# Gated delta layer, back stage: order of the gate weight loads on SyncE and of the state update on VectorE

## What is computed

```python
def step(s, xs):
    q_c, k_c, u_c, w_c, qk_c, sd_c = xs
    v_new = u_c - jnp.einsum('bhck,bhkv->bhcv', w_c, s)
    o_c = jnp.einsum('bhck,bhkv->bhcv', q_c, s) + jnp.einsum('bhij,bhjv->bhiv', qk_c, v_new)
    s = s * sd_c[..., None, None] + jnp.einsum('bhck,bhcv->bhkv', k_c, v_new)
    return s, o_c
...
gate = jax.nn.silu(z.reshape(bsz, t, GDN_V_HEADS, GDN_HEAD_V).astype(jnp.float32))
o = rms_norm(o, norm_w) * gate
```

## Time and profile before

| | us |
|---|---|
| median of 3 runs (lowest, highest) | 3392.73 (3389.57, 3393.57) |
| profiled execution, whole | 3392.64 |
| its span, first to last instruction | 3390.8 |

### The profile page before, as it was taken

The page is one execution under the profiler, slowest core; times in us unless marked ns, Lnnn a source line. Parts: engine busy times, 40 slices in busy tenths (PEclk is TensorE's granted clock), DMA queues, the critical chain, the costliest instruction groups (busy, mean ns, idle before and its releaser), DMA issues. The chain is left out here.

```text
span 3390.8 us, 41168 instructions
## 1 busy us (share of the span) xinstructions
PE 2907.4 (86%) x15594; PEld 2543.9 (75%) x15594; DVE 1855.7 (55%) x3342; ACT 1207.2 (36%) x2080; POOL 642.0 (19%) x386
## 2 busy tenths in 40 slices
PE   5787659969999999899999997998566768699987
PEld 4787438868898989898888886877455558588877
DVE  4324443327997988577788785449223333444433
ACT  3323442223225776333333333663133331222221
POOL 0002110002332333364233230430111110000000
PEclk8898789989999999999999998999778879899999
DMA  2102012133435888899999995572533322222222
GB/s 106 61 15 77 2 50 87 62 127 132 143 112 195 296 311 292 315 397 364 355 362 359 355 360 183 175 224 95 156 89 94 96 72 94 100 99 99 98 89 81
DMA packets 248691, 574.56 MB, mean 169 GB/s; under 512 B 43776, under 2 KB 152192, under 8 KB 217312
## 3 DMA queue, kind: packets, MB, share of 16 engines
q1 hardware_dynamic: 209808, 430.24, 37.8%
q0 software_dynamic: 36864, 134.23, 10.2%
q10 hardware_dynamic: 1872, 8.13, 0.7%
HBM read 486.39 MB, written 86.11 MB: 169 GB/s over the span
## 5 line engine op out<-in xcount | busy, mean ns | idle before, releaser
L40 PE MATMUL pe_ps<-hh,pe_uh 128*128 128x384 f32 x1024 | 352.5, 344 | 21.7 <-issue 17.7
L41 PE MATMUL pe_ps<-hl,pe_uh 128*128 128x384 f32 x1024 | 346.6, 338 | 0.0
L42 PE MATMUL pe_ps<-hh,pe_ul 128*128 128x384 f32 x1024 | 346.3, 338 | 0.0
L40 PE MATMUL pe_ps<-pe_vh,pe_whi 128*128 128x512 f32 x768 | 299.5, 390 | 3.0 <-DVE pe_vl L1498 3.0
L41 PE MATMUL pe_ps<-pe_vl,pe_whi 128*128 128x512 f32 x768 | 299.3, 390 | 0.0
L42 PE MATMUL pe_ps<-pe_vh,pe_wlo 128*128 128x512 f32 x768 | 299.3, 390 | 0.0
L1325 POOL DMA_INDIRECT pe_gu<-in_u_rows,pe_urow x128 | 198.2, 1548 | 316.4 <-DVE pe_gu L1459 289.8
L1333 POOL DMA_INDIRECT pe_gv<-in_v_w,pe_vrow x128 | 155.6, 1216 | 333.3 <-DVE pe_acc L1468 318.8
L40 PEld LDWEIGHTS pe_ps<-hh,pe_uh 128*128 128x128 f32 x1024 | 196.1, 191 | 24.0 <-issue 23.7
L40 PE MATMUL sc_ps<-hh,sc_wh 128*128 128x512 f32 x512 | 200.5, 392 | 13.0 <-DVE sc_wl L2695 13.0
L1459 DVE SCALAR_TENSOR_TENSOR pe_gu<-pe_gu,pe_xs 128x1024 f32<-128x1024 f32 x128 | 155.2, 1219 | 91.6 <-DMA pe_gu<-in_u_rows,pe_urow 91.2
(11 more groups left out here) (479 smaller groups left out, 7197.2 us busy)
## 6 DMA issues: line engine op xcount, KB each, us to landing
xu<-in_u_w SPq DMA_DIRECT2D x64, 1024.0 KB, 6.6
pe_v_raw<-in_v_w SPq DMA_DIRECT2D x64, 1024.0 KB, 8.4
sc_raw<-in_sc_w SPq DMA_DIRECT2D x32, 1024.0 KB, 4.9
hidden_scratch<-pe_hs SPq DMA_DIRECT2D x64, 384.0 KB, 8.9
gate_scratch<-pe_stage SPq DMA_DIRECT2D x24, 1024.0 KB, 11.1
pe_hw<-hidden_scratch SPq DMA_DIRECT2D x64, 384.0 KB, 4.7
pe_gate<-gate_scratch SPq DMA_DIRECT2D x64, 384.0 KB, 5.3
mrg_raw<-in_mrg_w SPq DMA_DIRECT2D x16, 1024.0 KB, 4.8
```

The lines of the kernel that those rows point to most:

```text
L40: pe.matmul(out, lh, rh, start=start, stop=False)
L41: pe.matmul(out, lh, rl, start=False, stop=False)
L42: return pe.matmul(out, ll, rh, start=False, stop=stop)
```

## The change

On SyncE, the load of gate weight tile 2 is issued at the end of the prologue, and the later ones two chunks sooner than before, at the head of an odd chunk's work in front of its two chunk loads. On VectorE, `state(1, g-1)` is issued in front of `merge`.

```diff
@@ gdn_back, block.sync
                     load_u(l, B)
                     load_rc(2 + l)
                     load_at(l, B)
+                load_z(2)
                 for g in range(LAST):
                     c, i = g // NCH, g % NCH
+                    if i % 2 and g // 2 + 3 < 2 * KH:
+                        load_z(g // 2 + 3)
                     if g + 3 < LAST:
                         load(0, g + 3)
                         load(1, g + 3)
-                    if i % 2 and g // 2 + 2 < 2 * KH:
-                        load_z(g // 2 + 2)
                     if g % B == 1 and 2 * B <= g + 7 < LAST:
@@ gdn_back, block.vector
                     rest(0, g)
+                    if g:
+                        state(1, g - 1)
                     if due(c, i) is not None:
                         merge(due(c, i))
-                    if g:
-                        state(1, g - 1)
                     rest(1, g)
```

## The result

The changed kernel takes 3277.0 us (median of 4 runs, 3273.09 to 3281.2) against 3391.43 us of the kernel before beside it (4 runs, 3389.57 to 3393.57). The ratio is 0.9663, 95% interval 0.9646 to 0.9679: 3.4% less, 114 us. The profiled execution has a span of 3273.0 us against 3390.8.

The account below looks back on a forecast made before the run. Late gate weights stalling ScalarE, and so TensorE, were taken as the bound: 3392.7 us less 109.6 (114.1 from idle time and lower clock, less 4.5 for a new `ub` wait) gave 3283 us, range 3273 to 3306.

Parts of the forecast that it names:

- The bound: ScalarE waits 89.1 us in 14 pieces at `high` for gate weights asked for too late, idling TensorE 70.9 us.
- The clock's part: In the back stage's loop, matmuls at the lower clock level after gaps cost 30 us, which would go.
- The rival by which the clock stays low: Only idle time in the loop goes, the 30 us of slower matmuls stay: 3313 us, chance 0.05.
- The loop without stalls: From `solve` of chunk 0 to that of chunk 31, 215.1 us instead of 329.2, summed from undisturbed stretches.
- two bare chunks: Two chunks without corner and merge took 11.10 us, so each chunk's base was put at 5.55 us.
- ScalarE's longest chain: After `gate`: `high`, table load, root, corner and hand-over take 3.2 us, ending 0.3 us before TensorE is ready for `merge`.
- rival (a): Other ScalarE and VectorE queue work replaces the stalls, 14 to 28 us back: 3297 to 3311 us, chance 0.20.
- The wait that appears: In chunk 2 of a head, merge waits for late `ub` loads: 1.3 to 3.1 us three times, 4.5 taken.
- Slower: Weights in front delay the chunk loads, TensorE waits at `carry` for `pk_in`: 3479 us for 25 us delay, chance 0.02.

Follow-up runs that it names:

- second set: The changed kernel run again unaltered, on the same chip as a kernel with ub loads in front and one scale moved: 3282.9 us, ratio 0.9676.
- edit 2: Only the VectorE swap, state in front of merge, against the kernel before, with the old load order: 3371.9 us, ratio 0.9958.
- edit 1 alone: Only the sooner gate weight loads against the kernel before, VectorE keeping merge in front of state: 3296.1 us, ratio 0.9738.

## Why the prediction was right, and where it was off

3283 us were predicted, within 3273 to 3306; 3277.0 were measured, and 3282.9 in the second set.

**The bound.** ScalarE's queue standing at `high` was the cause. One stall put back costs 8.0 us, and with edit 2 in place the 14 of them are worth 94.5 us of the loop.

**The clock's part,** 30 us: TensorE's waits fell by 90.7-13.1 = 77.6 us (the earlier trace rows against the list after) and the loop by 112.5, so the clock's part was 34.9 us, the fall of its busy time (238.27 to 203.35). The rival by which the clock stays low fell: 1.00. The premise behind it, that gaps up to 3.15 us leave the clock alone, holds only as far as it was needed: the longest gap in the loop now is 1.31 us, but with edit 1 alone one of 2.63 us was followed by a fall.

**The loop without stalls** was put at 215.1 us without the `ub` wait. The kernel with the `ub` loads in front is just that case: 212.6. That the two are so near is luck in part, since the terms of the sum were off in both directions. The two bare chunks of before, and the first of them in the changed kernel:

```profile
2733.60:2739.16 5.56, 5.56 (x34) 4.26 (x33) 2.61 (x8) 2.97 (x7) 0.36 (x1) 0.96 0.16 47
2739.16:2744.70 5.54, 5.16 (x35) 4.02 (x33) 3.42 (x11) 1.77 (x7) 2.01 (x1) 1.00 0.01 3
...
2614.87:2620.22 5.35, 5.35 (x35) 4.04 (x33) 2.61 (x8) 3.43 (x9) 0.36 (x1) 1.00 0.19 49
```

The first bare chunk wasn't undisturbed: it ran at 0.96 and takes 5.35 us now, so 31 x 0.2 = 6 us were too many. The second holds a `turn`, but it also lacks one step of the projection, which has run out by then (0.7 us), and that hid the cost of the `turn`: TensorE's next product starts 0.44 us behind its start, and 11 of them in the loop are 4.8 us that the sum doesn't have. A merge, corner or `within` was put at 0.94 us; chunk 1 takes 7.13 us now, so a pair costs 7.13-5.35 = 1.78, 0.89 each, and 41 x 0.05 = 2 us were too many. (Against its 8.66 us before, the wait of 1.26 us had cost 1.5.) The passage from one head to the next (chunks 7 and 8 take 6.00 and 7.48 us, their parts come to 7.13 and 8.02) saves 1.7 us three times, not 0.5 four times: 3 too many. And the waits for `r` and `pt` are 9.7 us in that kernel, not 6.5; among them is one that I had not, in chunk 4 of two heads the corner now waits 0.86 us for `pt`, where before one of the two waited 0.23 and the other not at all. With all this the sum is about 211 us; 1 to 2 us stay open.

**ScalarE's longest chain** was put 0.3 us ahead of `merge`; it ends 0.2 us ahead. No wait for `m1` came up in any chunk, so rival (a), with 14 to 28 us back, found nothing. The root follows the table load here, too: the load ends at 2477.03, the corner starts at 2477.28. The drain that the Trainium skill ("ScalarE: Activation LUTs", What ACT_TABLE_LOAD costs) adds, about 1.38 us, would as an estimate from that figure have moved it by 1.4 us and shown as a wait for `m1`; the trace has none.

**Edit 2** was put at the 13.3 us of its waits, in every chunk. Alone it gave 14 us in the whole and 18.0 in the loop, behind edit 1 it is worth 21.5 in the loop. Each time the waits are not all of it, and matmuls at the lower level are the rest (5.0 and 8.2 us). The `ub` wait was named by the same prediction, but I had not put the two together: without the swap the wait for `ub` reaches the state, and the clock falls.

**The wait that appears** was predicted in place, cause and size: 1.3 to 3.1 us three times, 1.5 taken; 1.3 measured, with `ub` landing in 2.4 to 2.5 us, the row that I had taken as nearer. The run behind the chunk loads, where `ub` follows the weights, landed it in 4.1 us and cost 4.0 to 4.5 a time. The Trainium skill ("DMA: Bandwidth & Descriptors", Queues, rings and completion order) says that each DMA engine takes the descriptors of a ring in order. That run agrees with it, as does the one with the `ub` loads in front of the chunk loads, where they too follow right behind the weights (3.8 us, against 2.4 with the chunk loads between). But in no kernel did `ub` stand in front of the weights, so whether the order is the reason or only that both are under way at once isn't shown.

**Slower,** by weights that hold up the chunk loads: with 832 KB in place of 512 there is still no such wait.

## What to carry to other kernels

On a queue with waits, a load belongs in front of every wait that it doesn't need itself; the waits passed were worth 90.7 us in the loop here, the two chunks of lead on top some 5, which the clock took back in that pair of kernels. A stall that goes uncovers the next late load, and one can find it beforehand by counting, from a common event, when each transfer is issued, when it lands and when its reader comes. Price a gap of TensorE with the matmuls that follow it: here 5.6 us idle cost 8.1.

## What I had not expected of the hardware

Gaps of nearly the same length did not have the same effect on the granted clock. With edit 1 alone the gaps in the three chunks 2 of a head were 2.87, 3.02 and 2.63 us long, and the granted clock of these chunks was 0.84, 0.72 and 0.84. With the weights in front only, gaps of 2.80, 2.75 and 2.72 us at the same places left it at 1.00 each time, and in the kernel before one of 3.15 us did so too. So the length of the gap alone doesn't decide: chunk 10 took 12.4 us in the one kernel and 9.6 in the other. What does decide is not shown here. And a wait of 1.26 us on TensorE cost 1.5 us with its clock at the upper level throughout.
